# Wider stage heads: four output blocks at a time instead of three, with the last input tile taken block by block

## The reference, cut to what matters

```python
h = concatenate([meta, x])                          # 272 x 1024
h = h + 0.5 * rmsnorm(swiglu(rmsnorm(h, g0), ffn_w_in[0], ffn_w_out[0]), g1)   # D_FF = 2816
h = h + rmsnorm(mlstm_mixer(rmsnorm(h, g2), ...), g3)
h = h + 0.5 * rmsnorm(swiglu(rmsnorm(h, g4), ffn_w_in[1], ffn_w_out[1]), g5)
x = h[16:]                                          # 256 x 1024
for l in (0, 1):
    u = rms_norm(x, pre[l]) * (1 + scale) + shift
    q, k, v, g_att, conv_inputs = split(u @ w_in[l])        # 1024 x 4096
    mix = concatenate([dilated_attention(q, k, v) * silu(g_att), gated_short_conv(...)])
    x = x + gate * rms_norm(mix @ w_out[l], post[l])
```

## Time and profile before

| | us |
|---|---|
| median of 3 runs (lowest, highest) | 839.85 (838.86, 840.29) |
| the profiled execution | 839.27 |
| its span, first to last instruction | 837.4 |

### The profile page before, as it was taken

The page is one execution under the profiler, slowest core; times in us unless marked ns, Lnnn a source line. Parts: engine busy times, 40 slices in busy tenths (PEclk is TensorE's granted clock), DMA queues, the critical chain, the costliest instruction groups (busy, mean ns, idle before and its releaser), DMA issues.

```text
span 837.4 us, 15752 instructions
## 1 busy us (share of the span) xinstructions
PE 809.7 (97%) x6455; PEld 783.0 (94%) x6455; DVE 586.0 (70%) x946; ACT 417.6 (50%) x716; POOL 128.7 (15%) x138
## 2 busy tenths in 40 slices
PE   7999999999999999999999999999999999999996
PEld 7999999999999899999999999989888998898895
DVE  6777776798687875797777768785666478466543
ACT  7444444544257565454444445445654355364542
POOL 3000000132210000110000012220235202025413
PEclk9999999999899999999999999999999999999998
DMA  9866777676245632568787775517445552744421
GB/s 330 296 239 223 227 252 234 231 265 203 84 152 184 189 121 78 156 221 318 270 290 276 270 237 179 184 43 251 150 128 148 153 176 64 238 129 149 129 76 51
DMA packets 45751, 158.96 MB, mean 190 GB/s; under 512 B 5064, under 2 KB 7624, under 8 KB 45680
## 3 DMA queue, kind: packets, MB, share of 16 engines
q1 hardware_dynamic: 45680, 157.96, 57.4%
HBM read 156.88 MB, written 1.06 MB: 189 GB/s over the span
## 4 chain that ended last, share of the span: by engine, by line
PE 78%; DVE 13%; ACT 6%; issue 2%; POOL 1%; DMA 0%; DVEq 0%; SPq 0%; ACTq 0%; POOLq 0%
PE ps L112 71%; PE ps L114 8%; DVE w L114 2%; DVE u L114 2%; ACT w L114 1%; DVE tmp L114 1%; DVE yg L114 1%; DVE Sb L114 1%; DVE st L114 1%; DVE cv L114 1%; ACT SW L114 1%; ACT Sb L114 1%; ACT ytm L114 1%; ACT L114 1%; POOL rst L114 1%
## 5 line engine op out<-in xcount | busy, mean ns | idle before, releaser
L112 PE MATMUL ps<-u,w 128*128 128x256 f32 (+1 forms) x3887 | 503.5, 286 | 3.2 <-ACT u L114 1.1
L112 PEld LDWEIGHTS ps<-u,w 128*128 128x128 f32 x3887 | 483.9, 189 | 12.9 <-DVE u L114 5.9
L114 DVE TENSOR_TENSOR w<-raw,w 128x1024 fp32r<-128x1024 f32 x245 | 297.9, 1225 | 170.1 <-ACT w L114 163.4
L114 ACT CAST w<-raw 128x1024 fp32r<-128x1024 f32 x245 | 255.3, 1051 | 132.1 <-PE ps L114 128.5
L112 PE MATMUL ps<-h,w 128*128 128x272 f32 (+1 forms) x1000 | 129.9, 285 | 0.0
L112 PEld LDWEIGHTS ps<-h,w 128*128 128x128 f32 x1000 | 126.0, 188 | 0.0
L114 POOL TENSOR_TENSOR sqa<-sqa,sq 128x256 f32<-128x256 f32 (+1 forms) x22 | 23.7, 1079 | 359.2 <-ACT sq L114 358.8
L114 POOL TENSOR_SCALAR Sb<-Sb,st 128x256 f32<-128x256 f32 x32 | 42.9, 1354 | 113.9 <-DVE st L114 113.9
L114 DVE SCALAR_TENSOR_TENSOR acc<-adr,cact,acc 128x1024 f32<-128x1024 f32 x42 | 56.6, 1358 | 0.1
L114 PE MATMUL ps<-u,w 128*128 128x256 f32 (+1 forms) x169 | 46.8, 285 | 0.0
L112 PE MATMUL ps<-m,w 128*128 128x256 f32 x368 | 46.4, 281 | 0.0
(11 more groups left out here) (175 smaller groups left out, 697.7 us busy)
## 6 DMA issues: line engine op xcount, KB each, us to landing
raw<-wst SPq DMA_DIRECT2D x245, 512.0 KB, 4.6
adr<-wada SPq DMA_DIRECT2D x48, 512.0 KB, 3.8
Bt<-bias_rows SPq DMA_DIRECT2D x8, 192.0 KB
hT<-xT SPq DMA_DIRECT2D x4, 272.0 KB, 4.5
outT<-hT SPq DMA_DIRECT2D x2, 384.0 KB, 2.6
outT<-hT SPq DMA_DIRECT2D x1, 256.0 KB, 2.6
cs<-cst SPq DMA_DIRECT2D x1, 140.0 KB, 5.9
cs<-cst SPq DMA_DIRECT2D x1, 128.0 KB, 6.7
```

Of the source, the lines that this page charges most:

```text
L112: fn()
L114: fn().then_inc(m[0], m[1])
```

## The change

`HB` goes from 3 to 4. In `head`, the first seven tiles in the order are done as before; the last tile is done block by block, with all three products of a block together, so that the blocks end one after another and not all at the end.

```diff
-        HB = 3
+        HB = 4
@@ head
-            for i, kt in enumerate(order):
+
+            order = list(order)
+            for i, kt in enumerate(order[:KT - 1]):
...
                 pe.wait(low[kt])
                 for b, c in zip(b_, c_):
-                    f = partial(nc.tensor.matmul, ps[:, b, 0:n], w1[:, c % NW, o:o + P], x2[:, kt, :], start=False,
-                                stop=i == KT - 1)
-                    if i < KT - 1:
-                        pe.quiet(f)
-                    else:
-                        m = pe(f)
-                        done_chunk(c, m)
-                        ready.append((b, m))
+                    pe.quiet(partial(nc.tensor.matmul, ps[:, b, 0:n], w1[:, c % NW, o:o + P], x2[:, kt, :],
+                                     start=False, stop=False))
+            if hook:
+                hook(KT - 1)
+            kt = order[KT - 1]
+            pe.wait(high[kt], low[kt])
+            for b, c in zip(b_, c_):
+                m = tile_products(ps[:, b, 0:n], c, kt, x1[:, kt, :], x2[:, kt, :], False, True, True)
+                done_chunk(c, m)
+                ready.append((b, m))
```

## The result

Thirteen executions of the changed kernel have a median of 843.13 us (839.98 to 843.93), thirteen of the kernel before 839.46 (838.76 to 840.29). The ratio is 1.0036, with a 95% interval of 1.0026 to 1.0047: +3.7 us in the median, where +2.0 was forecast. The executions now spread over 4 us, before over 1.5. The fastest one of each kernel in that comparison stand 1.2 us apart.

The account below looks back on a forecast made before the run. TensorE, busy 97%, bounds the kernel, so only its waits count. Stage terms -1.13 - 1.38 - 1.54 + 1.92 + 0.71 + 1.08 + 2.30 give +1.96 us: median 841.8 us, 8-in-10 range 838.4 to 845.2.

Parts of the forecast that it names:

- The fills and what is left of them: Feed-forward 2, layer 0 in, layer 1 in: tile waits of 2.07, 2.08, 2.08 us filled; net -1.13, -1.38, -1.54 us.
- The split of c+4: Layer 0 in and 1 in (c: head's first chunk): this split ends at 564.00 and 705.69 us, setting the next start.
- Mixer in's queue: Mixer in: the split of c+5 stands behind four evacuations; TensorE waits 2.45 us, net +1.92 us.
- The bank waits: Head starts of mixer out, layer 0 out, layer 1 out: waiting for the fourth bank costs +0.71, +1.08, +1.10 us.
- One sign that I had named for being wrong: Whole kernel: the forecast is wrong if the clock differs from before outside 219 to 227 us.
- The clock: Rival: mixer in's 2.45 us wait (or another) brings a new half-clock stretch, +3.5 us, 845.3 us; chance 0.14.
- the place named: The new 2.45 us wait in mixer in, where a half clock would follow by the skill's rule.
- The out stages of the layers: Layer 0 out +1.08 us for a bank; layer 1 out +2.30 us, a bank wait and a split wait of 1.2.
- Feed-forward 2's wait: Feed-forward 2: TensorE waits 0.78 us for the split of c+5, after starting c+4 0.15 us late; net -1.13 us.

Follow-up runs that it names:

- e4: Changed kernel with each block taken from `ready` also recording the split for its chunk number plus four; 840.74 us, ratio 1.0007.
- e2: Changed kernel with the heads of mixer out, layer 0 out and layer 1 out back to three blocks; 837.12 us, ratio 0.9968.

## Why the prediction came out as it did

Right, by its own steps:

- The fills and what is left of them: -1.13, -1.38 and -1.54 forecast, -1.16, -1.28 and -1.53 measured. The split of c+4, not the head's end, sets the next start in both layers' in stages; the DVE rows at 565.28 and 707.19 end 0.05 us ahead of TensorE's start.
- Mixer in's queue: two rounds of taps ahead of the split, a wait of 2.45 forecast and 2.22 measured. e4 shows that the queue is the cause: with the split ahead of the taps that wait is gone.
- The bank waits: 0.71, 1.08 and 1.10 forecast; 0.66, 1.02 and 1.02 measured as idle time. The heads of the layers' out stages started 1.19 us later behind the block ahead of them than before. e2 shows that the out stages only lose.

The direction and the order of size follow from these. One sign that I had named for being wrong did come true: the clock differs from before outside 219 to 227 us. Off in size, +3.9 for +1.96 in the traces:

- *The clock.* I gave the half clock the standing of a rival with 0.14 and +3.5 us. In the profiled execution it came at the place named, shorter, and cost 1.5 us, of which the mixer gave 0.4 back (TensorE's wait for the last `Vs`, 0.8 us before, is 0.4 now). Over executions it is no rival but a part of the median: the three of the thirteen with the highest clocks took 840.0 to 840.4, near what is forecast without it for a kernel whose fastest executions take 838.1 to 838.8, and ten took 841.9 to 843.9. I had also missed that mixer out's wait, grown to 2.2 us, is a second such place; I read its 1.7 before as a sign that waits of this length are harmless.
- *The out stages of the layers*, +1.59 and +2.70 for +1.08 and +2.30. A part is the head's start (1.19 for 1.08 and 1.10), and 0.1 us before each stage's head. The next is the pace. In their four-block heads a matmul costs (674.72 - 664.43) / 86 = 0.120 us; before, (670.12 - 662.02) / 69 = 0.117. Over 96 matmuls that is 0.2 us a head. In e2, with three blocks, it is 0.117 again (65 in 7.63 us). The rest is 0.1 us for the first block's bank behind the head, and small. I had carried the three-block pace over. The number of blocks is not the cause: the head of mixer out in the kernel before has three and is as slow, (331.89 - 326.82) / 42 = 0.121, and so are the single blocks behind layer 1 out's head, (820.60 - 817.81) / 23 = 0.121 and (824.65 - 821.84) / 23 = 0.122. The block after them is at 0.117 again. What these stretches share is a wait of TensorE shortly before. The granted clock is 1.00 in all; the cause is open. The row of the kernel before:

```profile
326.82 5.23 PE L112 MATMUL ps<-y,w 128*128 128x256 f32 x42
331.89 0.52 PE L114 MATMUL ps<-y,w 128*128 128x256 f32 x3
```

- *Feed-forward 2's wait* was 0.41, not 0.78: c+4 started 0.23 us behind the head's end (370.56 to 370.79) where I had 0.15, its matmuls were at the slow pace of 0.121 us too, and the split came no later than forecast. Together the term came out right.

## What to carry to other kernels

Widening a group of output blocks fills TensorE only where it waits for input tiles; look at each stage's own windows before giving all of them one width. A group that takes every rotating bank waits for the newest one's reader at its start, and work that is recorded only once the group's results are handed out (here the weight splits) lies behind all their evacuations: spread it between them. Price a wait of some 2 us on TensorE at its own length plus a chance of 3.4 us at half clock, which cost 1.5 us here. Before giving a small difference of two such kernels a cause, look at how much half clock each execution had.

## What I had not expected of the hardware

A half clock behind a wait as short as 1.8 to 2.2 us, in some profiles and not in others. And that fp32r matmuls of 256 columns, which start 0.117 to 0.118 us apart in most blocks, start 0.120 to 0.122 apart in the stretches behind a wait of TensorE, with four, three or one PSUM bank in turn, all at a granted clock of 1.00.
